# First inputs of the norm loaded a stage early, gates cast on ScalarE, rotary tables behind the first weights

## The chip, the core and the metric

The kernel runs on one core of a Trainium2 chip. The metric is device time in microseconds (us) of one launch, as the median of several runs. A profile shows one further execution. Engines are named as the profile names them: PE is TensorE (PEld its weight loads), DVE is VectorE, ACT is ScalarE, POOL is GpSimd, SP is SyncE, which only issues DMAs; SPq, ACTq and POOLq are DMA issues by these engines. L406 is line 406 of the kernel before.

## The reference, cut to what matters

Two transformer layers over 256 context rows and 1024 latent rows of width 1024, fp32 throughout. What the change touches is the modulation, the first norm, the projection, and the gates of the gated linear attention:

```python
for layer in range(DEPTH):
    m_lat = jnp.split((silu_c @ w_ada[layer] + b_ada[layer])[:, None, :], 6, axis=-1)
    m_ctx = jnp.split(silu_cc @ w_ada[layer] + b_ada[layer], 6, axis=-1)
    pl = project_heads(modulate(h_lat, m_lat[0], m_lat[1]) @ w_in[layer], ...)   # modulate: layer norm * (1 + scale) + shift
    pc = project_heads(modulate(h_ctx, m_ctx[0], m_ctx[1]) @ w_in[layer], ...)
    # in project_heads, per direction:
    gate = jax.nn.log_sigmoid((z @ w + b).astype(F32)) / GLA_GATE_NORM
    # rotary cos and sin are applied to the d_q, d_k, s_q, s_k columns only
    ...
    # three attentions (gla, diff, swa), out projection, post norm, swiglu
```

## The kernel before

The program is a row of stages with a barrier between each two: modulation; norm of the inputs; then per layer input projection (layer 1's follows layer 0's feed-forward), gated linear attention, differential attention, sliding-window attention, norm after attention, feed-forward. Within a stage each engine has its own instruction list, written by hand, and waits on semaphores. P is 128, D is 1024 and BANK is 512.

**Modulation** (`modulation`, L137). Six chunks of 512 columns of `w_ada` (2 MB each) go through a ring `W` of four buffers. SP issues a chunk (L160) and its four small bias pieces (L162); PE makes 32 small products of a chunk (L184); DVE adds the bias (L195); ACT sends the rows to the DRAM scratch `mod` (L171) and at the end waits for all of them.

**Norm of the inputs** (`norm_tiles` with kind "input"). Ten tiles of 128 rows. Step r of the software pipeline does on PE first the product of a `w_ada` chunk (L406, chunk r-1) and then the eight transposes of a tile (L414, tile r-1). SP loads chunk r (L350; from the third on after the product two earlier, since `aW` has two buffers), a bias row (L357) and tile r of the inputs into `hres` (L365, two buffers). DVE takes statistics (L432), ACT the deviation (L508), then normalizes (L514) for the transposes, then scales and shifts what PE turned (L528). The shift and scale columns come from `mod` by four POOL DMAs of single elements (L551); DVE waits for all four before anything else (L427), POOL too.

**Input projection** (`input_projection`). 21 weight tiles of 512 KB, two buffers: SP loads `raw` (L644), ACT casts it to the high part `whi` (L682), POOL subtracts for the low part `wlo` (L658), PE multiplies (L125 to L127 of the helper `product`). SP first issues the two rotary tables `cos` and `sin`, 1 MB each (L638, L639), and only then `raw`; POOL waits for both tables before its first subtraction. DVE uses them from tile 12 on.

**Gated linear attention** (`gated_linear_attention`). SP loads `zs` (six DMAs), then, once POOL has zeroed `wg`, its eight pieces (L925, L927), then `out` with the values (L928), the level tables into `X` (L929), keys and queries. PE makes five pairs of gate logits (L1016) in two PSUM buffers; ACT takes the absolute value (L1182) and DVE the minimum with 0 (L1296), which frees the buffer for the pair after next. DVE's list begins with the cast of the level tables (L1291). Then ACT does exp (L1185) and ln (L1188) of all five pairs; per pair j DVE subtracts (L1308, `g_done`) and casts the high part `ghi` (L1310), POOL makes the low part `glo` (L973). The distances (L1046, L1047) of piece k need `glo` of pair k, a free one of two `DP` buffers, and their exponentials (L1204) wait for all five `g_done`.

The few lines that set this order:

```python
# DVE, per pair j
dve.tensor_tensor(gate[:, j, :], gate[:, j, :], absx[:, j, :], ALU.subtract).then_inc(g_done, 1)
dve.wait_ge(g_done, j + 1)
dve.tensor_copy(ghi[:, 2 * j:2 * j + 2, :], gate[:, j, :]...).then_inc(ghi_done, 1)
# PE, distances: piece q waits for the exponential of piece q - 2
if q >= 2: pe.wait_ge(e_done, q - 1)
```

## Time and profile before

| | |
|---|---|
| three runs | 4027.97, 4030.92, 4032.74 us |
| median | 4030.92 us |
| the profiled execution | 4030.76 us; its span, first to last instruction, 4028.9 us |
| busy PE / POOL / DVE / ACT | 3537.6 / 1677.6 / 1615.7 / 1438.8 us (88 / 42 / 40 / 36%) |
| mean granted PE clock | 0.933 of full speed |
| modulation | 0 to 46.1 us, PE busy 18.3 |
| norm of the inputs | 46.1 to 148.4 us, PE busy 82.6 |
| input projection, layer 0 | 148.4 to 467.6 us, PE busy 292.4 |
| gated linear attention, layer 0 | from 467.6 us |
| input projection, layer 1 | 2268.5 to 2564.3 us |
| gated linear attention, layer 1 | from 2564.3 us |

The span is read stage by stage: between two barriers only the chain that ends last in a stage moves what follows. A timeline row gives the start of a piece of work, its length, and in brackets how long its engine sat idle before it and what released it.

### The profile page before, as it was taken

Reading aid. Unit: us, or ns where it says so; the run is one execution under the profiler, and the core shown is the slowest. Engines: PE = TensorE matmul, PEld = TensorE weight load, DVE = VectorE, ACT = ScalarE, POOL = GpSimd, SP = SyncE. Lnnn points to the kernel's source line nnn. Section 1 sums busy time; section 2 is a strip of 40 time slices with the busy share of each in tenths; the row PEclk is TensorE's granted clock in tenths of the full one; section 3 lists DMA queues with packets and bytes.
Section 4 is the critical chain, followed back from the end, with each engine's and each line's share of the span. In section 5 each row is a group of like instructions: output and inputs, shape, how many; then the busy total and the mean of one; then the engine's idle time right before and its main releaser. Section 6 shows DMA issues by size and latency. Waiting matters only on the chain. (4 is left out here: it accounts for less than half of the span.)

```text
span 4028.9 us, 54991 instructions
## 1 busy us (share of the span) xinstructions
PE 3537.6 (88%) x21518; PEld 2917.4 (72%) x21518; DVE 1615.7 (40%) x2566; ACT 1438.8 (36%) x2413; POOL 1677.6 (42%) x1108
## 2 busy tenths in 40 slices
PE   6799688698897999999999599597989879999997
PEld 2488578466576888888888488386665668888886
DVE  2103464585573222224433303564955722223324
ACT  2311265585543111113332211275854432222221
POOL 1211153493334444445555211243933345555553
PEclk8899789698998999999999799698999989999998
DMA  8422410231253222222333223312243533333332
GB/s 284 171 82 108 136 29 19 70 72 50 51 163 101 65 66 65 63 63 88 117 100 110 86 89 110 110 41 63 69 144 96 172 103 97 95 94 110 110 100 94
DMA packets 171083, 388.52 MB, mean 96 GB/s; under 512 B 14536, under 2 KB 75048, under 8 KB 170864
## 3 DMA queue, kind: packets, MB, share of 16 engines
q1 hardware_dynamic: 149184, 334.38, 27.2%
q10 hardware_dynamic: 19200, 44.63, 3.0%
q0 software_dynamic: 2480, 6.48, 0.6%
q8 instruction: 151, 2.47, 0.3%
q14 instruction: 68, 0.56, 0.0%
HBM read 319.41 MB, written 66.03 MB: 96 GB/s over the span
## 5 line engine op out<-in xcount | busy, mean ns | idle before, releaser
L2350 POOL TENSOR_TENSOR ffn_wlo<-ffn_raw,ffn_whi 128x1024 fp32r<-128x1024 f32 x264 | 644.5, 2448 | 680.8 <-ACT ffn_whi L2262 680.7
L2262 ACT CAST ffn_whi<-ffn_raw 128x1024 fp32r<-128x1024 f32 x264 | 272.6, 1049 | 879.0 <-PE ffn_acc L127 467.1
L2484 DVE TENSOR_TENSOR ffn_silu<-ffn_up,ffn_silu 128x256 f32<-128x256 f32 (+1 forms) x143 | 75.4, 528 | 946.3 <-PE ffn_up L127 937.0
L125 PE MATMUL ffn_gate<-second_uhi,ffn_whi 128*128 128x256 f32 (+1 forms) x1144 | 375.1, 328 | 42.9 <-POOL ffn_wlo L2350 34.3
L126 PE MATMUL ffn_gate<-second_ulo,ffn_whi 128*128 128x256 f32 (+1 forms) x1144 | 374.4, 327 | 0.0
L127 PE MATMUL ffn_gate<-second_uhi,ffn_wlo 128*128 128x256 f32 (+1 forms) x1144 | 374.1, 327 | 0.0
L125 PE MATMUL ffn_up<-second_uhi,ffn_whi 128*128 128x256 f32 (+1 forms) x1144 | 371.0, 324 | 0.9 <-POOL ffn_wlo L2350 0.9
L126 PE MATMUL ffn_up<-second_ulo,ffn_whi 128*128 128x256 f32 (+1 forms) x1144 | 370.8, 324 | 0.0
L127 PE MATMUL ffn_up<-second_uhi,ffn_wlo 128*128 128x256 f32 (+1 forms) x1144 | 370.4, 324 | 0.0
L2496 DVE TENSOR_TENSOR y<-ffn_acc,y 128x512 f32<-128x512 f32 x360 | 248.3, 691 | 260.3 <-PE ffn_acc L127 260.3
L125 PE MATMUL ffn_acc<-ffn_whi,ffn_hhi 128*128 128x512 f32 x792 | 315.0, 398 | 22.3 <-DVE y L2496 21.0
L126 PE MATMUL ffn_acc<-ffn_wlo,ffn_hhi 128*128 128x512 f32 x792 | 312.6, 395 | 0.0
L127 PE MATMUL ffn_acc<-ffn_whi,ffn_hlo 128*128 128x512 f32 x792 | 311.7, 394 | 0.0
L658 POOL TENSOR_TENSOR in_wlo<-in_raw,in_whi 128x1024 fp32r<-128x1024 f32 x42 | 100.2, 2389 | 454.1 <-ACT in_whi L682 454.1
L125 PEld LDWEIGHTS ffn_gate<-second_uhi,ffn_whi 128*128 128x128 f32 x1144 | 220.8, 193 | 64.4 <-POOL ffn_wlo L2350 35.1
L126 PEld LDWEIGHTS ffn_gate<-second_ulo,ffn_whi 128*128 128x128 f32 x1144 | 220.8, 193 | 19.1
L127 PEld LDWEIGHTS ffn_gate<-second_uhi,ffn_wlo 128*128 128x128 f32 x1144 | 220.7, 193 | 17.7
L125 PEld LDWEIGHTS ffn_up<-second_uhi,ffn_whi 128*128 128x128 f32 x1144 | 217.9, 190 | 18.9 <-POOL ffn_wlo L2350 1.5
L127 PEld LDWEIGHTS ffn_up<-second_uhi,ffn_wlo 128*128 128x128 f32 x1144 | 217.8, 190 | 17.3
L126 PEld LDWEIGHTS ffn_up<-second_ulo,ffn_whi 128*128 128x128 f32 x1144 | 217.9, 190 | 17.2
L2065 DVE TENSOR_SCALAR_CACHE_REDUCE diff_scores<-diff_scores 128x1280 f32<-128x1280 f32 (+1 forms) x144 | 196.8, 1384 | 34.9 <-PE diff_scores L1919 33.3
L125 PE MATMUL in_acc<-first_uhi,in_whi 128*128 128x512 f32 (+1 forms) x504 | 179.8, 357 | 20.7 <-POOL in_wlo L658 20.7
(285 smaller groups left out, 7980.1 us busy)
## 6 DMA issues: line engine op xcount, KB each, us to landing
ffn_raw<-w_ffn_dram SPq DMA_DIRECT2D x264, 512.0 KB, 3.6
in_raw<-w_in_dram SPq DMA_DIRECT2D x42, 512.0 KB, 3.6
norm_input_ada_w<-w_ada_dram SPq DMA_DIRECT2D x10, 2048.0 KB, 8.3
swa_ada_w<-w_ada_dram SPq DMA_DIRECT2D x8, 2048.0 KB
proj_scratch<-in_stage ACTq DMA_DIRECT2D x20, 640.0 KB, 2.9
ada_w<-w_ada_dram SPq DMA_DIRECT2D x6, 2048.0 KB
gla_kq<-proj_scratch SPq DMA_DIRECT2D x32, 320.0 KB
local_qhl<-heads_scratch SPq DMA_DIRECT2D x36, 256.0 KB
```

Of the source, the lines that this page charges most:

```text
L125: pe.matmul(out, st_hi, mv_hi, start=start, stop=False)
L126: pe.matmul(out, st_hi, mv_lo, start=False, stop=False)
L127: return pe.matmul(out, st_lo, mv_hi, start=False, stop=stop)
L658: pool.tensor_tensor(wlo[:, s, :, :], raw[:, s, :].rearrange("p (k n) -> p k n", k=KT), whi[:, s, :, :].bitcast(F32), ALU.subtract).then_i ...
L2065: dve.tensor_scalar(SC[:, c, 0:keys], SC[:, c, 0:keys], -scale, 3e38, ALU.mult, ALU.min, accum_out=ng[:, c:c + 1]).then_inc(neg_done, 1)
L2262: act.copy(whi[:, w % 3, :], raw[:, w % 2, :]).then_inc(w_hi, 1)
L2350: pool.tensor_tensor(wlo[:, w % 3, :], raw[:, w % 2, :], whi[:, w % 3, :].bitcast(F32), ALU.subtract).then_inc(w_ready, 1)
L2484: dve.tensor_tensor(sg[:, n % 2, 0:tn], UP[:, n % 2, 0:tn], sg[:, n % 2, 0:tn], ALU.mult).then_inc(mul_done, 1)
L2496: dve.tensor_tensor(Y[:, tt, cols], ACC[:, half, :], Y[:, tt, cols], ALU.add).then_inc(y_added, 1)
```

## The change

The kernel before is called before, the changed one after. The change has four parts.

First, new buffers `inputs_hres` and `inputs_ada_w` are allocated around modulation and norm. At the end of SP's list in modulation come the two context tiles (512 KB each) and the first two `w_ada` chunks of the norm (2 MB each). The norm no longer issues these four.

Second, in the input projection of both layers SP issues the first two weight tiles, then the two rotary tables, then the remaining weight tiles; from the second pair on in a loop, in layer 1 too, where they were unrolled. POOL's wait for the tables is gone.

Third, in the gated linear attention the eight pieces of `wg` are issued by ACT instead of SP.

Fourth, the cast `ghi` moves from DVE to ACT, one pair behind ln; the subtractions `glo` of pairs 1 and 3 move from POOL to DVE, and PE waits for `glo_pool` or `glo_dve`.

```diff
@@ -126,6 +126,16 @@
+
+
+def input_buffers(nc, ctx):
+    sb, _, sem = allocators(nc, ctx, "inputs_")
+    return {
+        "hres": sb("inputs_hres", [P, 2, D]),
+        "ada_w": sb("inputs_ada_w", [P, 2, KT, BANK]),
+        "h_in": [sem(f"h_in{s}") for s in range(2)],
+        "ada_in": [sem(f"ada_in{s}") for s in range(2)],
+    }
@@ -160,6 +170,11 @@
                     sp.dma_start(B[32 * j:32 * j + 2, n % 4, :], t["b_ada"][l:l + 1, part(c, j)].to_broadcast([2, P])).then_inc(w_in[n % 4], 16)
+            inputs = res["inputs"]
+            for s in range(2):
+                sp.dma_start(inputs["hres"][:, s, :], t["ctx"][s * P:(s + 1) * P, :]).then_inc(inputs["h_in"][s], 16)
+            for s in range(2):
+                sp.dma_start(inputs["ada_w"][:, s, :, :], t["w_ada"][1].rearrange("(k p) n -> p k n", p=P)[:, :, s * BANK:(s + 1) * BANK]).then_inc(inputs["ada_in"][s], 16)
@@ -228,7 +243,7 @@
         uhi, ulo, ident = res["uhi"], res["ulo"], res["ident"]
-        hres = sb(nm + "hres", [P, 2, D])
+        hres = sb(nm + "hres", [P, 2, D]) if post else res["inputs"]["hres"]
@@ -256,18 +271,18 @@
         if chunked:
-            aW = sb(nm + "ada_w", [P, 2, KT, BANK])
+            aW = res["inputs"]["ada_w"]
...
-        ada_in = [sem(f"ada_in{s}") for s in range(2)]
+        ada_in = [sem(f"ada_in{s}") for s in range(2)] if post else res["inputs"]["ada_in"]
...
         const_in, eps_set, one_plus = sem("const_in"), sem("eps_set"), sem("one_plus")
-        h_in = [sem(f"h_in{s}") for s in range(2)]
+        h_in = [sem(f"h_in{s}") for s in range(2)] if post else res["inputs"]["h_in"]
@@ -347,7 +362,7 @@
                         wait_apart(sp, product_done, chunk_count(i, r) - 2, sp_passed)
-                    sp.dma_start(aW[:, r % 2, :, :], columns).then_inc(ada_in[r % 2], 16)
+                        sp.dma_start(aW[:, r % 2, :, :], columns).then_inc(ada_in[r % 2], 16)
@@ -361,8 +376,9 @@
-                    wait_count(sp, summed if post else normed[1], count(i, r) - 2)
-                    sp.dma_start(hres[:, s, :], src_rows(i, s)).then_inc(h_in[s], 16)
+                    if post or not isinstance(i, int) or count(i, r) > 2:
+                        wait_count(sp, summed if post else normed[1], count(i, r) - 2)
+                        sp.dma_start(hres[:, s, :], src_rows(i, s)).then_inc(h_in[s], 16)
@@ -635,14 +651,14 @@
         def _(sp):
-            sp.dma_start(cos[:, :, :], t["rope_cos"].rearrange("a p n -> p a n")).then_inc(rope_in, 16)
-            sp.dma_start(sin[:, :, :], t["rope_sin"].rearrange("a p n -> p a n")).then_inc(rope_in, 16)
-
...
                 sp.dma_start(raw[:, s, :], t["w_in"][layer][bass.ds(n * P, P), :]).then_inc(raw_in[s], 16)
-            each_tile(sp, body)
+            each_tile(sp, body, 0, 1, False)
+            sp.dma_start(cos[:, :, :], t["rope_cos"].rearrange("a p n -> p a n")).then_inc(rope_in, 16)
+            sp.dma_start(sin[:, :, :], t["rope_sin"].rearrange("a p n -> p a n")).then_inc(rope_in, 16)
+            each_tile(sp, body, 1)
@@ -651,7 +667,6 @@
                 pool.dma_start(t["heads"][part, HEAD_SK:HEAD_SK + P, T:PAD_T], zero[:, :]).then_inc(pad_out, 16)
-            pool.wait_ge(rope_in, 32)
@@ -825,7 +840,7 @@
         logits, abs_done, exp_of_abs, log_done = sem("logits"), sem("abs_done"), sem("exp_of_abs"), sem("log_done")
-        g_done, ghi_done, glo_done = sem("g_done"), sem("ghi_done"), sem("glo_done")
+        g_done, ghi_done, glo_pool, glo_dve = sem("g_done"), sem("ghi_done"), sem("glo_pool"), sem("glo_dve")
@@ -919,12 +934,6 @@
                 sp.dma_start(zs[base + GATE_RANK:base + 2 * GATE_RANK, 0:1], proj[rows, T - 1:T]).then_inc(load["z"], 16)
-            sp.wait_ge(wg_zero, 1)
-            for base in (0, 64):
-                for d in range(2):
-                    sp.dma_start(wg[base + d * GATE_RANK:base + (d + 1) * GATE_RANK, :, d, :],
-                                 t["w_gate"][layer, d].rearrange("r (h k) -> r h k", h=H)).then_inc(load["w"], 16)
-                    sp.dma_start(wg[base + 32:base + 33, :, d, :], t["b_gate"][layer, d:d + 1, :].rearrange("a (h k) -> a h k", h=H)).then_inc(load["w"], 16)
@@ -968,10 +977,10 @@
             pool.wait_ge(zeroed, 2)
-            for j in range(PAIRS):
+            for j in range(0, PAIRS, 2):
...
                 pool.tensor_tensor(glo[:, 2 * j:2 * j + 2, :], gate[:, j, :].rearrange("p (c n) -> p c n", c=2),
-                                   ghi[:, 2 * j:2 * j + 2, :].bitcast(F32), ALU.subtract).then_inc(glo_done, 1)
+                                   ghi[:, 2 * j:2 * j + 2, :].bitcast(F32), ALU.subtract).then_inc(glo_pool, 1)
@@ -1040,7 +1049,7 @@
                     if g == 0:
-                        pe.wait_ge(glo_done, c // 2 + 1)
+                        pe.wait_ge(glo_dve if c // 2 % 2 else glo_pool, c // 4 + 1)
@@ -1177,15 +1186,29 @@
         def _(act):
+            act.wait_ge(wg_zero, 1)
+            for base in (0, 64):
+                for d in range(2):
+                    act.dma_start(wg[base + d * GATE_RANK:base + (d + 1) * GATE_RANK, :, d, :],
+                                 t["w_gate"][layer, d].rearrange("r (h k) -> r h k", h=H)).then_inc(load["w"], 16)
+                    act.dma_start(wg[base + 32:base + 33, :, d, :], t["b_gate"][layer, d:d + 1, :].rearrange("a (h k) -> a h k", h=H)).then_inc(load["w"], 16)
...
                 act.activation(absx[:, j, :], absx[:, j, :], ACT.Exp, scale=-1.0).then_inc(exp_of_abs, 1)
+
+            def high_part(j):
+                act.wait_ge(g_done, j + 1)
+                act.copy(ghi[:, 2 * j:2 * j + 2, :], gate[:, j, :].rearrange("p (c n) -> p c n", c=2)).then_inc(ghi_done, 1)
+
...
                 act.activation(absx[:, j, :], absx[:, j, :], ACT.Ln, bias=1.0).then_inc(log_done, 1)
+                if j:
+                    high_part(j - 1)
+            high_part(PAIRS - 1)
@@ -1306,8 +1329,10 @@
                 dve.tensor_tensor(gate[:, j, :], gate[:, j, :], absx[:, j, :], ALU.subtract).then_inc(g_done, 1)
-                dve.wait_ge(g_done, j + 1)
-                dve.tensor_copy(ghi[:, 2 * j:2 * j + 2, :], gate[:, j, :].rearrange("p (c n) -> p c n", c=2)).then_inc(ghi_done, 1)
+                if j >= 2 and j % 2 == 0:
+                    dve.wait_ge(ghi_done, j)
+                    dve.tensor_tensor(glo[:, 2 * j - 2:2 * j, :], gate[:, j - 1, :].rearrange("p (c n) -> p c n", c=2),
+                                      ghi[:, 2 * j - 2:2 * j, :].bitcast(F32), ALU.subtract).then_inc(glo_dve, 1)
@@ -2545,14 +2570,16 @@
         everything = list(range(TILES))
-        modulation(nc, t, res)
...
                     operand(ctx, "first")
-                    norm_tiles(nc, t, res, "input", layer, everything, False)
+                    with nc.cleanup_on_exit(), ExitStack() as inputs:
+                        res["inputs"] = input_buffers(nc, inputs)
+                        modulation(nc, t, res)
+                        norm_tiles(nc, t, res, "input", layer, everything, False)```

SP, from the last chunk of modulation into the norm, before:

```order
L160 DMA ada_w<-w_ada_dram 128x8x512
L162 DMA ada_b<-b_ada_dram 2x128 x4
L134 UNCONDITIONAL_BRANCH
L332 UNCONDITIONAL_BRANCH
L350 DMA norm_input_ada_w<-w_ada_dram 128x8x512
L365 DMA norm_input_hres<-ctx_dram 128x1024
L350 DMA norm_input_ada_w<-w_ada_dram 128x8x512
L357 DMA norm_input_ada_b<-b_ada_dram 2x512
L365 DMA norm_input_hres<-ctx_dram 128x1024
```

and after:

```order
L170 DMA ada_w<-w_ada_dram 128x8x512
L172 DMA ada_b<-b_ada_dram 2x128 x4
L175 DMA inputs_hres<-ctx_dram 128x1024 x2
L177 DMA inputs_ada_w<-w_ada_dram 128x8x512 x2
L144 UNCONDITIONAL_BRANCH
L347 UNCONDITIONAL_BRANCH
L372 DMA norm_input_ada_b<-b_ada_dram 2x512
L365 DMA inputs_ada_w<-w_ada_dram 128x8x512
```

The branches are the stage's end and the next one's start: four large loads have moved ahead of them, and the first large load of the norm is now its third chunk.

ACT, from the start of the gated linear attention of layer 0 to its first exponentials, before:

```order
L1178 UNCONDITIONAL_BRANCH
L1182 ACTIVATE gla0_E<-gla0_unit 128x1024 x5
L1185 ACT_TABLE_LOAD
L1185 ACTIVATE gla0_E<-gla0_E 128x1024 x5
L1188 ACT_TABLE_LOAD
L1188 ACTIVATE gla0_E<-gla0_E 128x1024 x5
L1204 ACT_TABLE_LOAD
L1204 ACTIVATE gla0_E<-gla0_dist 128x2x2x128 x13
```

and after, from the load of the table for ln on:

```order
L1208 ACT_TABLE_LOAD
L1208 ACTIVATE gla0_E<-gla0_E 128x1024 x2
L1204 CAST gla0_ghi<-gla0_XAB 128x1024
L1208 ACTIVATE gla0_E<-gla0_E 128x1024
L1204 CAST gla0_ghi<-gla0_XAB 128x1024
L1208 ACTIVATE gla0_E<-gla0_E 128x1024
L1204 CAST gla0_ghi<-gla0_XAB 128x1024
L1208 ACTIVATE gla0_E<-gla0_E 128x1024
L1204 CAST gla0_ghi<-gla0_XAB 128x1024 x2
L1227 ACT_TABLE_LOAD
L1227 ACTIVATE gla0_E<-gla0_dist 128x2x2x128 x13
```

`gla0_XAB` holds the gates and `gla0_E` the logarithms. The five casts now stand between the logarithms and ahead of the table for the exponentials; no further table load has come in.

## Rows read from the trace of the kernel before

**Rows 1.** Timeline, modulation to norm: start, length (us), work [idle before <-releaser].

```profile
25.63 4.59 SPq L162 DMA_DIRECT2D ada_b<-b_ada_dram  x4
...
43.18 1.16 ACTq L171 DMA_DIRECT2D mod_scratch<-ada_rows  x4
...
46.12 0.39 SPq L350 DMA_DIRECT2D norm_input_ada_w<-w_ada_dram  x1
...
49.51 0.88 POOL L551 DMA_DIRECT2D norm_input_scale<-mod_scratch  x1
...
56.65 9.50 PE L406 MATMUL norm_input_ada_acc<-norm_input_ada_w,silu_c 128*2 128x512 f32 x16 [14.82 <-DMA norm_input_ada_w<-w_ada_dram]
56.67 0.17 DVE L427 TENSOR_SCALAR norm_input_scale<-norm_input_scale 128x16 f32<-128x16 f32 x1 [13.53 <-DMA norm_input_scale<-mod_scratch]
...
57.92 1.29 DVE L432 BATCH_NORM_STATS2 norm_input_stats<-norm_input_hres 128x6 f32<-128x512 f32 x2 [1.08 <-DMA norm_input_hres<-ctx_dram]
...
61.68 1.24 ACT L514 ACTIVATE norm_input_x<-norm_input_hres,norm_input_nmu,norm_input_rstd 128x1024 f32<-128x1024 f32 x1 [0.42 <-DVE norm_input_nmu L445]
...
66.08 1.09 PE L414 MATMUL norm_input_tr<-ident,norm_input_x 128*128 128x128 f32 x8
...
67.10 7.03 PE L406 MATMUL norm_input_ada_acc<-norm_input_ada_w,silu_c 128*2 128x512 f32 x16
```

**Rows 2.** Table of stretches, DMA alone busy: stretch, then busy times, PEclk, DMA share, GB/s.

```profile
30.00:35.00 5.00, 2.83 (x76) 2.07 (x72) 1.15 (x4) 0.00 (x0) 0.00 (x0) 0.84 1.05 405
```

**Rows 3.** Timeline, TensorE after a pause in the norm after attention.

```profile
1129.96 0.76 PE L125 MATMUL norm_attention_y<-norm_attention_wohi,norm_attention_mhi 128*128 128x512 f32 x1 [2.44 <-POOL norm_attention_mlo L564]
```

**Rows 4.** Timeline, start of both input projections; last, landing of their weights.

```profile
148.42 0.41 SPq L638 DMA_DIRECT2D in_cos<-rope_cos_dram  x1
...
158.02 1.04 ACT L682 CAST in_whi<-in_raw 128x1024 fp32r<-128x1024 f32 x1 [14.13 <-DMA in_raw<-w_in_dram]
...
161.62 0.79 PE L125 MATMUL in_acc<-first_uhi,in_whi 128*128 128x512 f32 x1 [20.67 <-POOL in_wlo L658]
...
2278.24 1.04 ACT L682 CAST in_whi<-in_raw 128x1024 fp32r<-128x1024 f32 x1 [13.59 <-DMA in_raw<-w_in_dram]
...
DMA to landing us min/median/max: 3.4/3.6/9.5
```

**Rows 5.** Timeline, start of the gated linear attention, layer 0.

```profile
470.29 0.74 SPq L925 DMA_DIRECT2D gla_wg<-w_gate_dram  x1
...
475.75 0.44 SPq L928 DMA_DIRECT2D gla_out<-proj_scratch  x1
...
476.94 3.79 PE L1016 MATMUL gla_unit<-gla_wg,gla_z 33*128 33x512 f32 x8 [22.93 <-DMA gla_wg<-b_gate_dram]
...
483.41 0.76 DVE L1291 CAST gla_levels<-gla_X 128x1152 fp32r<-128x1152 f32 x1 [21.41 <-DMA gla_X<-gla_levels_dram]
...
484.42 2.35 DVE L1296 TENSOR_SCALAR gla_XAB<-gla_unit 128x1024 f32<-128x1024 f32 x2
```

**Rows 6.** Timeline, its gates; last row, the same place in layer 1.

```profile
499.48 1.28 ACT L1188 ACT_TABLE_LOAD   x1
500.77 4.84 ACT L1188 ACTIVATE gla_E<-gla_E 128x1024 f32<-128x1024 f32 x5
501.94 1.22 DVE L1308 TENSOR_TENSOR gla_XAB<-gla_XAB,gla_E 128x1024 f32<-128x1024 f32 x1 [3.07 <-ACT gla_E L1188]
...
508.94 2.71 DVE L1310 CAST gla_ghi<-gla_XAB 128x1024 fp32r<-128x1024 f32 x1
...
516.70 1.08 ACT L1204 ACTIVATE gla_E<-gla_dist 128x512 f32<-128x512 f32 x2 [6.77 <-DVE gla_XAB L1308]
...
519.51 2.34 POOL L973 TENSOR_TENSOR gla_glo<-gla_XAB,gla_ghi 128x1024 fp32r<-128x1024 f32 x1 [0.63 <-DVE gla_ghi L1310]
...
522.00 0.55 PE L1046 MATMUL gla_dist<-gla_levels,gla_ghi 128*128 128x256 f32 x1 [1.78 <-POOL gla_glo L973]
...
2618.70 0.55 PE L1046 MATMUL gla_dist<-gla_levels,gla_ghi 128*128 128x256 f32 x1 [1.78 <-POOL gla_glo L973]
```

1 line of the change is left out of this document (added).

## The prediction, made before the changed kernel was run

> **What bounds the kernel now.** I read the table of stages first: nearly everything is a stage in which PE is busy nine tenths of the time, and the change touches none of that work. It touches three kinds of stage starts, where PE idles, so I read the timeline there. At the start of the norm of the inputs PE waits 14.82 us for its first chunk of weights and starts at 56.65, with the stage open since 46.12; DVE waits until 56.67 for the shift and scale columns [rows 1]. At the start of a projection ACT casts the first weights at 158.02, 9.6 us after SP's first issue at 148.42, because 2 MB of tables went ahead, and PE starts at 161.62 [rows 4]. At the start of the linear attention DVE waits until 483.41 for the level tables and PE until 476.94 for the gate weights [rows 5]; then a pair of gates costs DVE a subtraction of 1.22 and a cast of 2.71 while POOL works beside it, and the last low part starts only at 519.51 [rows 6]. The reader is to see that each wait ends a chain that the whole stage hangs on.
>
> **Norm of the inputs.** Removed: four loads of 5 MB from the stage's start. They now follow the sixth chunk on SP's queue. The DMA engines move 405 GB/s there [rows 2]. The first six chunks hold 12.6 MB and, at that rate from about 6 us on, are through by 37 (an estimate from that rate); 5.2 MB more take 12.9 us, so the queue drains at about 49.8, and the first chunk of the norm, 1 MB of tiles ahead of it, is there at about 45. SP finished its issues at 30.22 and the stage ended after 43 [rows 1], so SP has 12 us for four more. The six chunks stand ahead in the queue and are not delayed.
>
> What is delayed are the last rows that ACT sends at 43.18 to 44.34; the next stage opened 1.8 us after that [rows 1]. They now land beside a running 2 MB load. Bounds: 0, and about 5 us, from the columns that POOL issued until 50.39 and that came at 56.67 beside a load, 6.28 us, against the 1.8 or less that the rows take now [rows 1]. I take 1.2, near the short end, since the rows are eight descriptors and the columns thousands.
>
> In the norm PE can take its first chunk at once: 46.3 + 9.50 = 55.8. The first transposes need the columns too. POOL still issues them until 50.39. Lower bound for their landing is some 1.8 us more, as for the rows; upper bound is 56.67 as now. I take 53.0: the load beside them is gone by 49.8. From there the chain measured from the statistics at 57.92 to the end of the normalization at 61.68 + 1.24 is 5.0, and the addition ahead of it 0.2: 58.2. With the 1.2 us of the rows that is 59.4 where the row of the first transposes has 66.08: a gain of 6.7. Everything later in the stage follows at PE's pace: chunk of 7.03 and transposes of 1.09, and the third chunk is issued when the first product ends, 9 us before PE wants it, as now.
>
> PE then pauses 2.4 us between its first chunk and the transposes, where before it went straight on. The chunk in the granted clock's lower level (1.2 GHz of 2.4) took 9.50 against 7.03, so one more fall costs up to 2.5 [rows 1]. After a pause of 2.44 us elsewhere PE came back with a first product of 0.76 us, slow [rows 3]. I charge 1.2, between 0 and 2.5. **Term: 6.7 - 1.2 = 5.5, between 0 and 9.**
>
> **Input projection, both layers.** The first weight tile takes the place of the tables at 148.42. Landing takes 3.4 to 3.6 us where nothing is ahead [rows 4]: 152.0 instead of 158.02. The second follows 1.3 later, as now. The tables then land at about 158.5; POOL no longer waits for them, DVE first uses them twelve tiles later, and the third weight tile, issued when POOL has finished its first at about 155.6, lands behind them at 160, while PE has two tiles of some 14 us each to do (292.4 us for 21). The loop that replaces unrolled issues costs SP nothing that is seen: SP waits for POOL there. **Term: 6.0 in each layer, 12.0; between 5 and 6.5 each.** The rows of layer 1 are the same, 9.7 after the issue.
>
> **Linear attention, first half, both layers.** Eight issues leave SP's list: 475.75 - 470.29 = 5.46 us [rows 5]. `out` and the level tables are issued and land that much earlier, 483.41 becomes 478.0, and DVE's first minimum 484.42 becomes 479.0. For that the absolute value of pair 0 must be there, 3.1 us after PE's start (half of PE's 3.79 for two pairs and about 1 each for ACT and the hand-overs [rows 5]). ACT issues the eight pieces at the same 0.68 each from about 468.2 to 473.6, and PE starts 1.2 after the last one now: 474.9, or 475.5 with a little contention. The gain is whole as long as PE starts by 475.9. Here the row shows eight issues that hold up all behind them for 5.4 us. The Trainium skill says in "DMA: Bandwidth & Descriptors", "Issuing engines are not separate DMA queues", that issuing on several engines "will only save the time on the sequencer it takes to initiate the DMA, which is usually small relative to the DMA itself". By that sentence this half would bring next to nothing; the row speaks against it, as these pieces hold only a few KB. **Term: 5.4 in each layer, 10.8.**
>
> **Second half, both layers.** Counted from the first ln at 500.77 [rows 6]. Now the pairs follow at DVE's 1.2 + 2.7 = 3.9 each and the last low part ends at 519.51 + 2.34 = 21.1. After: an ln is 0.97 and a cast on ACT 1.04, as for the weights [rows 4]. ACT does ln 0, ln 1, then cast 0 when the first subtraction is there at 2.4; so cast 0 ends at 3.5, cast 1 at 5.5, cast 2 at 7.55, cast 3 at 9.6, cast 4 at 10.95 (its subtraction ends at 9.85). DVE has two low parts of 1.22, ending at 7.05 and 11.1; POOL three of 2.34, the last from 11.0 to 13.4. Then the load of the table for exp, which lay in a pause, stands behind cast 4: 1.28, so the first exponential starts at 12.25 against 516.70, that is 15.9. Three more pieces follow in PE's steps of 1.2: the last piece of the first step starts at 15.25, where the row has 522.00, that is 21.2. What is late next is PE itself, as pieces wait for a `DP` buffer, not the low part (13.4). Gain 5.95, and layer 1 has the same row, 2618.70. Bounds: 1, if ACT's casts take the 2.71 that DVE's took (rival b), and 6.5. **Term: 5.9 in each layer, 11.8.**
>
> Whether ACT's cast stays at 1.04 beside DVE and POOL has no row here; the cast of the weights, taken while no other engine worked, is the nearest in kind.
>
> **Sum.** 5.5 + 12.0 + 10.8 + 11.8 = 40.1. Against the profiled execution, 4030.76 us: 3990.7. The median of the runs is 4030.92, the same; I say 3990.7.
>
> **Rivals.** (a) Small transfers suffer beside the large ones. For it: the columns' 6.28 us [rows 1]. If the gate weights take that after 473.6, PE starts at 479.9 and the first half brings 1.4 instead of 5.4 in each layer: 8 us less. If the last rows of modulation take 5, 3.8 less. Both: 4002.5; one: 3995 to 3999. Against it: the pieces of `wg` have few descriptors, and now land 1.2 after their last issue though `out` is issued right behind them [rows 5]. The Trainium skill, in "DMA: Bandwidth & Descriptors", "Queues, rings and completion order", says that an engine drains a whole packet of one queue before it turns to the next; that would be such a delay, and no row here shows its size.
>
> (b) ACT is the new bound in the gates. If its casts took 2.71 as DVE's did, a pair would cost 0.97 + 2.71 = 3.7 against 3.9 and the second half would bring about 1 in each layer: 4000.5. A smaller form: the table load has to wait for the cast to drain. The rows show none: the load at 499.48 has no idle time of ACT ahead of it, right behind the five exponentials, and ln starts as its 1.28 are over [rows 6]. If a drain as long as the load came behind the cast, 1.28 in each layer, the time would be 3993.3. The Trainium skill, "ScalarE: Activation LUTs", "What ACT_TABLE_LOAD costs", counts about 1.38 us of drain with every switch; by that 3993.5.
>
> (c) The early loads buy nothing, because the columns bound the norm's start as they do now (56.67 against 56.65): the chain then gives 56.67 + 5.2 + 1.2 = 63.1, the first term is about 2, and the time 3994.
>
> (d) Slower. The granted clock moves against the change: PE's busy stretches of the feed-forward, 2000 us long, start in another phase. One fall costs 2.5 us at most [rows 1]. To lose the 40 us and 8 more it takes 20 more falls than now; with 24 the time is 4050.7. Nothing in the profile ties such falls to a shift of a whole stage.
>
> **How the numbers follow.** A difference of 0.2%, 8 us, is about what a measurement of this kernel tells from none. Forecast, 3985 to 3995: 0.70. (a) 0.09, (b) 0.08 (of it 0.03 for the small form), (c) 0.08, (d) 0.02, and 0.03 for a loss that has no place here. The forecast, (c), the small form of (b) and part of (a) lie within 3983 to 4001, which I take as the range. All but (d) and the unplaced loss are faster: 0.95 faster, 0.03 the same, 0.02 slower.
>
> **What would show it.** In the profile after: first product of the norm within 0.5 us of the stage's opening, first transposes 7 us earlier; modulation ending by about 47; first cast of weights 3.6 us after SP's first issue in both projections; first minimum of the gates 5.4 earlier after the stage's opening; five casts on ACT of about 1.04; first exponential some 11.5 us after the first ln. I am wrong if the next stage after modulation opens beyond 49, if the gate logits start later than 8.5 us after the stage opens, or if DVE and ACT wait for each other in the gates so that the first exponential comes later than 14 us after the first ln.

## The result and the profile after

The changed kernel takes 4001.62 us (median of four runs, 3997.66 to 4006.36) where the kernel before takes 4030.45 (four runs): 28.8 us less, ratio 0.9929 with a 95% interval of 0.9912 to 0.9946. The profiled execution of after took 4000.35 us with a span of 3998.6. The forecast was 3990.7, a gain of 40.1. The direction is right; more than a quarter of the gain is missing, and the time lies just beyond the upper end of the range, 4001. In all runs compared here the mean granted clock of TensorE was 0.93 to 0.94 of full speed; the one run far below that, at 0.725 and 4630.99 us, belongs to the last kernel of the experiments and is left out of its median.

Two lists find the missing part. The first is the length of each stage, from barrier to barrier, in the profiled executions:

| us | modulation | norm | projection 0 | linear attention 0 | projection 1 | linear attention 1 | all other stages | span |
|---|---|---|---|---|---|---|---|---|
| before | 46.1 | 102.3 | 319.2 | 251.2 | 295.8 | 212.7 | 2801.6 | 4028.9 |
| after | 49.8 | 93.4 | 312.6 | 244.2 | 289.7 | 208.7 | 2800.2 | 3998.6 |

The stage of the linear attention is over 200 us long and its later part moves by some us from run to run with the granted clock: the unaltered after kernel, profiled once more, had 249.5 where this table has 244.2, with the same gates. From DVE's first weighing to the stage's end it took 199.1 us at a mean granted clock of 0.90 there, and 193.0 us at 0.94 here. So the second list reads fixed places in it, in us after the stage opened (POOL's first row):

| us after opening, layer 0 / layer 1 | before | after |
|---|---|---|
| PE's first gate product | 9.3 / 9.8 | 12.2 / 11.6 |
| DVE's first minimum | 16.8 / 16.8 | 15.3 / 14.8 |
| ACT's first ln | 33.2 / 33.2 | 31.7 / 31.1 |
| ACT's first exponential of the distances | 49.1 / 49.1 | 46.7 / 46.1 |
| DVE's first weighing of keys and queries | 56.3 / 56.2 | 51.1 / 50.6 |

The gain, term by term: norm 5.2 (predicted 5.5), projections 6.6 + 6.1 (predicted 12.0), first half of the gates 1.5 + 2.0 (predicted 10.8; to the first minimum), second half 3.6 + 3.6 (predicted 11.8; from the first ln to the first weighing). The sum is 28.6, of the 30.3 by which the two profiled spans differ and beside 28.8 in the medians. That it comes so near is in part luck. In layer 0 the stage is 7.0 shorter, more than the 5.1 gained at the weighing, and in the second profile of after only 1.7; in layer 1, 4.0 of the 5.6 gained at the weighing are left at the stage's end. What is missing against the forecast stands in the two terms of the linear attention.

**Norm.** Timeline of after where [rows 1] are of before: start, length, work, and in brackets the idle time before it and its releaser.

```profile
26.48 18.43 ACTq L186 DMA_DIRECT2D mod_scratch<-ada_rows  x16
...
49.79 0.10 POOL L562 MEMSET norm_input_eps<- 128x1 f32 x1 [49.33 <-POOLq L144]
49.83 9.98 PE L422 MATMUL norm_input_ada_acc<-inputs_ada_w,silu_c 128*2 128x512 f32 x16 [7.43 <-PEq L144]
...
53.17 0.88 POOL L567 DMA_DIRECT2D norm_input_scale<-mod_scratch  x1
56.09 0.17 DVE L443 TENSOR_SCALAR norm_input_scale<-norm_input_scale 128x16 f32<-128x16 f32 x1 [12.37 <-DMA norm_input_scale<-mod_scratch]
...
61.22 1.09 PE L430 MATMUL norm_input_tr<-ident,norm_input_x 128*128 128x128 f32 x8 [1.41 <-ACT norm_input_x L530]
...
62.24 7.03 PE L422 MATMUL norm_input_ada_acc<-inputs_ada_w,silu_c 128*2 128x512 f32 x16
```

PE starts 0.04 us after the stage opens instead of 10.5. The columns land 2.04 after their last issue is over (53.17 + 0.88 to 56.09), against 6.28 before beside a load. The price is ahead of it: the last rows of modulation are issued until 44.91 and the stage ends 4.88 later; before, that was 1.78. The transposes are at 61.22, 4.9 earlier than in [rows 1].

**Projection.** The same view where [rows 4] are of before:

```profile
143.22 0.85 SPq L657 DMA_DIRECT2D in_raw<-w_in_dram  x2
...
147.16 1.04 ACT L697 CAST in_whi<-in_raw 128x1024 fp32r<-128x1024 f32 x1 [8.85 <-DMA in_raw<-w_in_dram]
```

The first cast comes 3.94 us after SP's first issue, where it came 9.60 after it; in layer 1 it is 4.36 (2245.82 to 2250.18), where it was 9.7. PE starts 5.7 and 5.4 earlier after the opening. The rest of the 6.6 and 6.1 lies in the products themselves, 291.54 us in all instead of 292.39 and 263.44 instead of 264.20; the granted clock in PE's first 20 us was 0.90 and 0.91 against 0.85 and 0.87 before.

**Start of the linear attention.** The same view where [rows 5] are of before, and then the table of stretches (busy time of PE, PEld, DVE, ACT and POOL, then clock, DMA share and GB/s) of the time in which PE waits:

```profile
458.86 0.49 SPq L937 DMA_DIRECT2D gla_out<-proj_scratch  x1
...
459.39 0.72 SPq L938 DMA_DIRECT2D gla_X<-gla_levels_dram  x1
...
460.16 5.34 SPq L943 DMA_DIRECT2D gla_kq<-proj_scratch  x8
...
461.25 0.64 ACTq L1194 DMA_DIRECT2D gla_wg<-b_gate_dram  x1
...
467.06 0.76 DVE L1314 CAST gla_levels<-gla_X 128x1152 fp32r<-128x1152 f32 x1 [16.84 <-DMA gla_X<-gla_levels_dram]
...
467.96 3.79 PE L1025 MATMUL gla_unit<-gla_wg,gla_z 33*128 33x512 f32 x8 [25.74 <-DMA gla_wg<-b_gate_dram]
...
471.13 1.22 DVE L1319 TENSOR_SCALAR gla_XAB<-gla_unit 128x1024 f32<-128x1024 f32 x1 [2.98 <-ACT gla_E L1197]
```

```profile
461.00:463.00 2.00, 0.00 (x0) 0.00 (x0) 0.00 (x0) 0.00 (x0) 0.00 (x0) 0.50 0.96 389
463.00:465.00 2.00, 0.00 (x0) 0.00 (x0) 0.00 (x0) 0.00 (x0) 0.00 (x0) 0.50 1.01 407
```

ACT has issued the last piece of `wg` at 461.89, but PE starts at 467.96, 6.07 later; in layer 1 5.7 later (2541.41 to 2547.12). In [rows 5] it was 1.2. In between the DMA engines are full, with values, levels, keys and queries at 389 to 407 GB/s; before, while the last pieces were issued (474 to 476), they were nearly idle at 13 GB/s. In the seven profiles whose linear attention starts with these lists the 6.07 is 5.6 to 6.3, and 4.6 to 5.8 in layer 1. What DVE waits for is no longer the level tables but ACT's absolute value, behind PE. The tables are cast 11.3 us after the opening, 4.6 earlier than before, where the prediction had 10.4.

**Gates.** Where [rows 6] are of before: after on DVE, then ACT, then POOL.

```profile
488.65 2.36 DVE L1331 TENSOR_TENSOR gla_XAB<-gla_XAB,gla_E 128x1024 f32<-128x1024 f32 x2 [3.08 <-ACT gla_E L1208]
492.01 2.54 DVE L1331 TENSOR_TENSOR gla_XAB<-gla_XAB,gla_E 128x1024 f32<-128x1024 f32 x1 [1.00 <-ACT gla_E L1208]
494.48 1.21 DVE L1334 TENSOR_TENSOR gla_glo<-gla_XAB,gla_ghi 128x1024 fp32r<-128x1024 f32 x1
495.61 4.50 DVE L1331 TENSOR_TENSOR gla_XAB<-gla_XAB,gla_E 128x1024 f32<-128x1024 f32 x2
```

```profile
487.49 2.00 ACT L1208 ACTIVATE gla_E<-gla_E 128x1024 f32<-128x1024 f32 x2
...
496.86 1.05 ACT L1204 CAST gla_ghi<-gla_XAB 128x1024 fp32r<-128x1024 f32 x1 [0.27 <-DVE gla_XAB L1331]
500.14 1.04 ACT L1204 CAST gla_ghi<-gla_XAB 128x1024 fp32r<-128x1024 f32 x1 [2.24 <-DVE gla_XAB L1331]
501.21 1.28 ACT L1227 ACT_TABLE_LOAD   x1
502.50 1.08 ACT L1227 ACTIVATE gla_E<-gla_dist 128x512 f32<-128x512 f32 x2
```

```profile
491.13 2.35 POOL L982 TENSOR_TENSOR gla_glo<-gla_XAB,gla_ghi 128x1024 fp32r<-128x1024 f32 x1 [30.72 <-ACT gla_ghi L1204]
495.71 3.32 POOL L982 TENSOR_TENSOR gla_glo<-gla_XAB,gla_ghi 128x1024 fp32r<-128x1024 f32 x1 [2.23 <-ACT gla_ghi L1204]
```

The casts on ACT take the predicted 1.04, and no idle time stands between the last one and the table load. But DVE's third subtraction takes 2.54 instead of 1.22, and the fourth and fifth together 4.50. Laid over POOL's rows, the lengths add up to taking turns: POOL works from 491.13 to 493.48, and DVE's subtraction that began at 492.01 ends at 494.55, about 1.1 after that. POOL's next, 3.32 long, begins 0.10 after a subtraction of DVE; 3.32 is about the rest of that subtraction (1.0) and 2.34. The last cast waits 2.24 for DVE, and the first exponential comes 15.0 us after the first ln, where 12.25 was predicted and 15.9 stood before.

A far smaller instruction, in the norm of the same trace, shows that this is waiting and not working at half speed:

```profile
74.07 2.33 DVE L461 SCALAR_TENSOR_TENSOR norm_input_nmu<-norm_input_mv,norm_input_rstd 128x1 f32<-128x1 f32 x1
74.04 2.34 POOL L585 TENSOR_TENSOR first_ulo<-norm_input_x,first_uhi 128x1024 fp32r<-128x1024 f32 x1 [5.56 <-DVE first_uhi L496]
```

It has one element per partition and takes 0.16 in the median of its ten; here it ends within 0.02 us of POOL's subtraction. Not every DVE instruction waits: the addition at 66.28, with one operand in PSUM, takes 0.68 while POOL subtracts from 66.14 to 68.48, and 0.67 at 76.32, where POOL is done.

### The profile page after: what moved, and what is told of

Read it like the earlier page. It is cut to its first block and busy times, and to the rows that moved or that the text cites. A ratio compares the mean times of both kernels' runs of the same rounds, so it can differ in the third digit from the quotient of the medians.

```text
span 3998.6 us, 55066 instructions
## 1 busy us (share of the span) xinstructions
PE 3531.9 (88%) x21518; PEld 2912.4 (73%) x21518; DVE 1602.3 (40%) x2560; ACT 1449.1 (36%) x2423; POOL 1662.3 (42%) x1104
## 5 line engine op out<-in xcount | busy, mean ns | idle before, releaser
L125 PE MATMUL ffn_gate<-second_uhi,ffn_whi 128*128 128x256 f32 (+1 forms) x1144 | 375.4, 328 | 42.8 <-POOL ffn_wlo L2375 34.1
L125 PE MATMUL ffn_up<-second_uhi,ffn_whi 128*128 128x256 f32 (+1 forms) x1144 | 370.9, 324 | 0.8 <-POOL ffn_wlo L2375 0.8
L125 PE MATMUL ffn_acc<-ffn_whi,ffn_hhi 128*128 128x512 f32 x792 | 314.1, 397 | 22.4 <-DVE y L2521 21.2
L125 PEld LDWEIGHTS ffn_gate<-second_uhi,ffn_whi 128*128 128x128 f32 x1144 | 221.0, 193 | 64.3 <-POOL ffn_wlo L2375 34.9
L125 PEld LDWEIGHTS ffn_up<-second_uhi,ffn_whi 128*128 128x128 f32 x1144 | 217.8, 190 | 18.9 <-POOL ffn_wlo L2375 1.5
L2068 POOL TENSOR_TENSOR diff_w<-diff_w,diff_e 128x1280 f32<-128x1280 f32 (+1 forms) x72 | 192.0, 2666 | 6.0
```

The costliest lines, as they stand in the source:

```text
L125: pe.matmul(out, st_hi, mv_hi, start=start, stop=False)
L2068: pool.tensor_tensor(w, w, E[:, u % 4, 0, 0:keys], ALU.add).then_inc(w_done, 1)
```

## Experiments

Each is an edit of the changed kernel. Times of a single run are given beside the run of before on the same chip; since runs of one and the same kernel lie up to 13 us apart (3996.44 to 4009.6 below), the places in the stages decide, and the time only supports them.

Two theories stand behind the first five; a third, of the same kind as T for the last rows of modulation, is called M in the expectations. **T**: the pieces of `wg` and other small transfers land late because large loads run beside them, not because of their engine or their count. **P**: a DVE instruction of two SBUF operands (or DVE's cast) and a POOL subtraction exclude each other; ACT's casts have no part in it. The rivals are in the expectations.

### Gate weights issued by SP again

```diff
 # SP, ahead of the load of the values; removed from ACT's list
+            sp.wait_ge(wg_zero, 1)
+            for base in (0, 64):
+                for d in range(2):
+                    sp.dma_start(wg[...], t["w_gate"][...]).then_inc(load["w"], 16)
+                    sp.dma_start(wg[...], t["b_gate"][...]).then_inc(load["w"], 16)
```

> The changed kernel with one part undone: SP issues the eight pieces of wg again, ahead of out and the level tables. Both theories expect the two linear-attention stages to open as they did before up to the first gates: PE's first logits 9.3 us and DVE's first minimum 16.8 us after the stage opens (after: 12.2 and 15.3; layer 1: 11.6 and 14.8). Theory T (the pieces on ACT land late because they run beside the loads that now start 5.4 us earlier): the move is worth 1.5 to 2 us in each layer, time 3 to 4 us above the changed kernel. Rival (the move is worth what the prediction gave it and something else in the stage ate it): 5.4 in each layer, 11 us above.

Measured: 4002.9 us (before 4029.84). PE's first gate product comes 9.5 and 9.4 after opening, the first minimum 17.1 and 17.2, against 15.3 and 14.8 in after. The third part of the change is worth 1.7 and 2.4 us, not 5.4. Over the seven profiles that have its lists, the minimum comes 14.7 to 15.7 and 13.7 to 15.2 after opening, so it is worth 1.4 to 2.4 and 2.0 to 3.5.

### Gate weights landed before the large loads start

```diff
+            sp.dma_start(X[:, 2, 0:tables * P].rearrange("p (l n) -> p l n", n=P), t["gla_levels"]).then_inc(load["lv"], 16)
+            sp.wait_ge(load["w"], 128)
             sp.dma_start(out[:, :, :], proj[T_GV * P:(T_GV + 2) * P, 0:T].rearrange("(i p) n -> p i n", p=P)).then_inc(load["v"], 16)
-            sp.dma_start(X[:, 2, 0:tables * P].rearrange("p (l n) -> p l n", n=P), t["gla_levels"]).then_inc(load["lv"], 16)
```

> The changed kernel, but SP issues the level tables before out and then waits until the eight pieces of wg have landed before it issues out, keys and queries; nothing large runs beside the pieces but the 0.6 MB of tables. Theory T (contention of the pieces with out and keys on the DMA engines): PE's first logits 7.4 to 8.4 us after the stage opens instead of 12.2, first minimum at about 10.5 to 11.5 instead of 15.3, some 4 us less in each layer, 8 in all. Rival (ACT's queue lands its pieces 6 us late whatever runs beside them): first logits stay at about 12, first minimum at 15, and out and keys come later, so the time rises by 0 to 4 us.

Measured: 3992.38 us (before 4029.84). Its timeline:

```profile
459.74 0.64 ACTq L1195 DMA_DIRECT2D gla_wg<-b_gate_dram  x1
461.54 0.76 DVE L1315 CAST gla_levels<-gla_X 128x1152 fp32r<-128x1152 f32 x1 [12.69 <-DMA gla_X<-gla_levels_dram]
462.15 0.39 SPq L939 DMA_DIRECT2D gla_out<-proj_scratch  x1
...
462.22 3.78 PE L1026 MATMUL gla_unit<-gla_wg,gla_z 33*128 33x512 f32 x8 [21.37 <-DMA gla_wg<-b_gate_dram]
```

The same eight pieces, from the same engine, land 1.84 us after the last issue (460.38 to 462.22) instead of 6.07, with only the 0.6 MB of level tables beside them; in layer 1 it is 2.4. The first minimum is at 11.0 and 11.4 after opening. That is T, and 5.9 and 5.4 earlier than in before: the size that was predicted for this half, by another order. The weighing is at 46.8 and 47.2 (51.1 and 50.6 in after), so the later keys and queries cost nothing.

### Casts on DVE and low parts on POOL again

```diff
-                if j >= 2 and j % 2 == 0:
-                    dve.wait_ge(ghi_done, j)
-                    dve.tensor_tensor(glo[pair j - 1], ...).then_inc(glo_dve, 1)
+                dve.wait_ge(g_done, j + 1)
+                dve.tensor_copy(ghi[:, 2 * j:2 * j + 2, :], gate[:, j, :].rearrange("p (c n) -> p c n", c=2)).then_inc(ghi_done, 1)
```

ACT's `high_part` is gone, and POOL makes all five low parts.

> The changed kernel with the fourth part undone: casts on DVE, all five low parts on POOL. From the first ln: first exponential at 15.9 us and DVE's first weighing at 23.1 as before (after: 15.0 and 19.45). Theory P (DVE's subtractions and POOL's low parts take turns, so the gates' chain is the sum of both engines' work; the cast alone left it): the part is worth 3.6 us at the first weighing and 3 to 4.5 at each stage's end, time 6 to 9 us above the changed kernel. Rival (it is worth the 5.9 of the prediction, hidden by noise of the clock): 12 us above.

Measured: 4014.78 us (before 4029.84), that is 14.4 above the profiled run of after, where 6 to 9 were expected: the stages of the linear attention are 5.7 and 4.3 longer, the others, which the edit doesn't touch, 4.4. The 5.7 shows nothing of the edit, as the second profile of after has the same length, 249.5 against 249.8 here. From the first ln to the first exponential it is 15.9 again and to the weighing 23.1, against 15.0 and 19.5 in after; the fourth part is worth 3.6 in each layer. DVE's and POOL's rows of this kernel:

```profile
489.71 0.69 DVE L1326 CAST gla_ghi<-gla_XAB 128x1024 fp32r<-128x1024 f32 x1
490.32 1.22 DVE L1324 TENSOR_TENSOR gla_XAB<-gla_XAB,gla_E 128x1024 f32<-128x1024 f32 x1
491.58 2.72 DVE L1326 CAST gla_ghi<-gla_XAB 128x1024 fp32r<-128x1024 f32 x1
```

```profile
490.58 3.16 POOL L982 TENSOR_TENSOR gla_glo<-gla_XAB,gla_ghi 128x1024 fp32r<-128x1024 f32 x1 [30.15 <-DVE gla_ghi L1326]
...
506.03 2.34 POOL L982 TENSOR_TENSOR gla_glo<-gla_XAB,gla_ghi 128x1024 fp32r<-128x1024 f32 x1 [0.63 <-DVE gla_ghi L1326]
```

Here the cast that [rows 6] show with 2.71 is seen without POOL beside it: 0.69. The 2.72 of the next one is the wait until POOL ends at 493.74 and then 0.56. POOL's 3.16 is about the rest of DVE's subtraction (0.9) and 2.34.

### All low parts on DVE

```diff
 # DVE, behind the subtraction of pair j; POOL makes none
+                for k in [[], [0], [1], [2], [3, 4]][j]:
+                    low_part(k)
```

> The changed kernel with all five low parts on DVE, the low part of pair j-1 behind the subtraction of pair j, none on POOL. Theory P (a DVE subtraction of two SBUF operands and a POOL subtraction take turns): every DVE subtraction and low part takes 1.22 us, none 2.5 to 4.5; the casts on ACT stay 1.04. By the lists then the first exponential comes 13.35 us after the first ln (15.0 in the changed kernel) and DVE's first weighing about 17.8 after it (19.45). Rival A (what stretches DVE's subtractions is ACT's cast or ln beside them, reading the same tiles): subtractions of 2.5 us and more remain, the first exponential 15 or later. Whole time 3997 to 3999 by P, 4002 or more by A, beside what the clock adds.

Measured: 3995.3 us (before 4030.67). DVE's rows:

```profile
487.61 2.36 DVE L1332 TENSOR_TENSOR gla_XAB<-gla_XAB,gla_E 128x1024 f32<-128x1024 f32 x2 [3.07 <-ACT gla_E L1204]
489.95 1.23 DVE L1326 TENSOR_TENSOR gla_glo<-gla_XAB,gla_ghi 128x1024 fp32r<-128x1024 f32 x1
491.09 1.22 DVE L1332 TENSOR_TENSOR gla_XAB<-gla_XAB,gla_E 128x1024 f32<-128x1024 f32 x1
492.23 1.22 DVE L1326 TENSOR_TENSOR gla_glo<-gla_XAB,gla_ghi 128x1024 fp32r<-128x1024 f32 x1
```

With POOL silent all twenty DVE instructions of the two layers take 1.22 to 1.23, with ACT's casts among them. The first exponential is 12.8 after the first ln, the weighing 17.25, each half a us sooner than expected. P holds and A falls. DVE does three instructions more than in after and is done sooner.

### Low parts on DVE, out of the way of the subtractions

```diff
+                for k in [[], [], [0], [], [1, 2, 3, 4]][j]:
+                    low_part(k)
```

> The changed kernel with all five low parts on DVE, but only that of pair 0 among the subtractions (behind subtraction 2), the other four behind subtraction 4, so that no low part stands ahead of a subtraction that ACT waits for. Theory P: first exponential 12.25 us after the first ln, the number that was predicted for the changed kernel (15.0 in it); DVE's first weighing 16.8 to 17.0 after it (19.45); PE's last piece of the first step at about 15.3. Rival A (ACT's casts stretch DVE's subtractions): as the changed kernel, 15.0 and 19.4. Whole time by P about 5 less than the changed kernel, 3996, beside what the clock adds; by A 4001.

Measured: 3994.79 us (before 4030.67). First exponential 11.95 after the first ln, the weighing 16.4 after it, in both layers. The prediction's schedule for ACT (12.25) is right once nothing excludes DVE.

### One weight chunk of the norm loaded in modulation

```diff
-            for s in range(2):
+            for s in range(1):
                 sp.dma_start(inputs["ada_w"][:, s, :, :], ...).then_inc(inputs["ada_in"][s], 16)
 # norm, SP: chunk 1 is issued at the stage's start again
```

> The changed kernel, but only the two context tiles and the first chunk are loaded in modulation; the second chunk (2 MB) is issued at the start of the norm. After: modulation ends at 49.8, first transposes at 61.2, norm ends at 143.2. Theory M (the last rows of modulation land late because 2 MB more are still in the queues): the queue drains at about 45, modulation ends at 46.5 to 47.3; the columns are slowed beside the second chunk and land at 53 to 55; first transposes at 58.5 to 60.5, norm ends 1 to 2.7 us earlier than 143.2. Rival (the end of modulation moved for another reason, such as the added instructions or the new buffers): modulation still ends at about 49.8 and the norm ends later than 143.2.

Measured: 4002.97 us (before 4029.84). Modulation ends at 47.64, 2.1 earlier than in after; but its last row was issued until 43.14, 1.8 earlier, and still lands 4.5 after that. The expected end of 46.5 to 47.3 was missed. In the norm:

```profile
47.64 0.38 SPq L367 DMA_DIRECT2D inputs_ada_w<-w_ada_dram  x1
...
51.03 0.88 POOL L569 DMA_DIRECT2D norm_input_scale<-mod_scratch  x1
...
57.78 0.17 DVE L445 TENSOR_SCALAR norm_input_scale<-norm_input_scale 128x16 f32<-128x16 f32 x1 [15.83 <-DMA norm_input_scale<-mod_scratch]
...
62.91 1.97 PE L432 MATMUL norm_input_tr<-ident,norm_input_x 128*128 128x128 f32 x8 [6.54 <-ACT norm_input_x L532]
64.81 8.65 PE L424 MATMUL norm_input_ada_acc<-inputs_ada_w,silu_c 128*2 128x512 f32 x16
```

Beside this one load the columns land 5.87 after their last issue instead of 2.04. PE then stood idle 6.54 us (1.41 in after), and its transposes and second chunk are slow, 1.97 and 8.65 against 1.09 and 7.03. The norm takes 100.5 and ends at 148.1 instead of 143.2; 1 to 2.7 us earlier than 143.2 was expected. Both chunks ahead of the norm are the better choice in spite of the rows.

### Only the tiles loaded in modulation

```diff
-            for s in range(2):
-                sp.dma_start(inputs["ada_w"][:, s, :, :], ...).then_inc(inputs["ada_in"][s], 16)
 # norm, SP: both chunks are issued at the stage's start again
```

> The changed kernel with only the two context tiles (1 MB) loaded in modulation; both weight chunks of the norm are issued in the norm again. Theory M (the last rows of modulation land late because large loads still run beside them): the queue drains by about 40, the last rows are issued by 44.3 as before, modulation ends at 46.1 (46.12 before, 49.79 in the changed kernel). Rival N (the lag is that of the end of the stage with two more buffers or semaphores, not of a load): 49 or more. The norm's start then is as before: first product 10 us after opening, columns beside a load 10.5 after opening, norm about 102 long, so the sum of modulation and norm about 148.2 against 143.2 in the changed kernel; whole time about 4006.

Measured: 4008.41 us (before 4030.67). The last row is issued until 43.31 and modulation ends at 45.1, 1.8 later, as in before, with the two new buffers in place: so it is the weight loads that hold the rows up, and N falls. PE starts at 55.69, 10.6 after opening; the transposes come at 64.99, and the norm takes 102.8. Modulation and norm sum to 147.9 (143.2 in after, 148.4 before).

### Both repairs together, beside the changed kernel

The edits of the second and the fifth experiment in one kernel; the changed kernel once more; and the former with the second weight chunk issued by SP in the norm once the columns have landed (`sp.wait_ge(const_in, const_loads)` ahead of it).

> The changed kernel unaltered, timed beside the two that follow, on the same chip. Every theory expects 4001 to 4002.

> The changed kernel with both repairs: SP issues the level tables first and waits for the gate weights before it issues the values, keys and queries; and all low parts on DVE, that of pair 0 behind subtraction 2 and the rest behind subtraction 4. If the two losses are separate and add, DVE's first weighing comes 4.0 earlier by the first (51.1 to 46.8 and 50.6 to 47.2 after the stage's opening) and 3.0 earlier by the second (19.45 to 16.4 after the first ln): 43.8 and 44.2 after the opening, and the whole time is 2 times 7 under the changed kernel: 3987 to 3989. Rival: the second gain is eaten by keys and queries that now land too late for the weighing; then weighing stays at 46 or later and the time at 3991 to 3994.

> As combined, and only the first weight chunk of the norm is loaded in modulation; SP issues the second in the norm once the four column loads have landed. Theory M (rows of modulation and columns of the norm each suffer from the large load beside them): modulation ends at 47.6 as with one chunk, the columns land 2.0 after the last issue as in the changed kernel, the second chunk is there before PE has turned the first tile, so the sum of modulation and norm is 141.2 against 143.2 in the changed kernel and 148.1 with one chunk issued at once. Rival: the second chunk comes too late, PE waits for it, and the sum is 143 or more. Whole time 2 under combined, or the same.

| | median us | runs | ratio to before on the same chip, 95% interval |
|---|---|---|---|
| before | 4027.24 | 9, 4025.59 to 4034.77 | |
| the changed kernel again | 4001.95 | 5, 3996.44 to 4009.6 | 0.9929, 0.9915 to 0.9942 |
| both repairs | 3989.03 | 4, 3986.89 to 3989.9 | 0.9898, 0.9883 to 0.9913 |
| and one chunk late | 3995.86 | 4, 3988.21 to 3998.11 | 0.9914, 0.9898 to 0.9929 |

With both repairs every run is faster than the fastest of the changed kernel (3989.9 against 3996.44); the medians are 12.9 us apart and the weighing is at 43.7 and 44.0 after opening, where 43.8 and 44.2 were expected. The losses were separate and add; this version beats both kernels.

The last variant missed. Modulation ends at 47.5 and the columns land 2.2 after their last issue, as expected, but:

```profile
53.89 0.38 SPq L368 DMA_DIRECT2D inputs_ada_w<-w_ada_dram  x1
...
56.65 0.37 SPq L365 DMA_DIRECT2D inputs_ada_w<-w_ada_dram  x1
...
59.00 0.35 SPq L384 DMA_DIRECT2D inputs_hres<-x_dram  x1
...
62.07 8.59 PE L425 MATMUL norm_input_ada_acc<-inputs_ada_w,silu_c 128*2 128x512 f32 x16 [1.95 <-DMA inputs_ada_w<-w_ada_dram]
...
68.83 1.29 DVE L451 BATCH_NORM_STATS2 norm_input_stats<-inputs_hres 128x6 f32<-128x512 f32 x2 [4.07 <-DMA inputs_hres<-x_dram]
```

The chunk lands 8.2 after its issue, with the third chunk sent after it at 56.65, and the third tile waits behind both and is 9.8 under way. The norm takes 97.8, 3.6 more than with both repairs alone (94.2), while modulation gained 2.1: the rival of that expectation, 145.2 for the sum against 143.8.

## Why the prediction came out as it did

**Norm: the sum right, two sizes in it off.** The step "I take 1.2, near the short end, since the rows are eight descriptors" failed: modulation ends 3.67 later, of which 0.57 is later issuing and 3.10 the landing. The reason given, few descriptors, decided nothing. Against it the clock's fall, charged at 1.2, did not come: PE paused 1.41 where 2.4 was predicted, and the second chunk took 7.03 at a granted clock of 1.00. Other profiles of the same lists had the predicted pause and more, 2.88 and 2.91, and the chunk took 7.03 all the same. The slow product after 2.44 us, [rows 3], did not carry over to this place. The columns landed 6.30 after opening (6.7 predicted), and from there to the transposes it was 5.1 (5.2). Net 5.2 for 5.5: that it is so near is luck, as the two errors, 2.5 too little for the rows and 1.2 too much for the clock, stand against each other and against a few tenths elsewhere. Rival (c), columns as late as 56.67, did not happen in its sense: they gate the start, but come 2.04 after the issue.

**Projection: right.** 6.6 and 6.1 for 6.0 each, with the 6.6 a little beyond the term's 6.5. The first cast alone moved by 5.7 and 5.3, and PE's start by 5.7 and 5.4; the 0.85 and 0.76 by which the products were shorter, beside a higher granted clock, were no part of the sum. That POOL, SP's loop and the later tables would cost nothing was right too. The clue was that both chains, [rows 4], had only one thing in front.

**Linear attention, first half: the mechanism right, the landing mis-sized.** SP issues `out` 5.1 us earlier after the opening, and the levels are cast 4.6 and 4.3 earlier, 5.4 by the prediction. The failed step is "PE starts 1.2 after the last one now: 474.9, or 475.5 with a little contention". The 1.2 was measured at a time when nothing large was under way (13 GB/s): on one queue, `wg` stood ahead of `out`. The change put `out`, levels, keys and queries in flight before the last `wg` piece. With 6.07 and 5.7 in the place of 1.2, this half is worth 1.5 and 2.0 instead of 5.4. It is rival (a), which had the size of layer 0 almost exactly: 1.4. It was given 0.09, against its own evidence of 6.28 in [rows 1]. The Trainium skill's sentence in "DMA: Bandwidth & Descriptors", "Issuing engines are not separate DMA queues", that a second issuing engine saves usually little beside the DMA itself, came nearer to this outcome (1.7 and 2.4 us by the first experiment) than the prediction's row did; yet the issue time was not small, 5.4, and the second experiment got all of it. What cost it was the order of arrival. The Trainium skill, in the same page's section "Queues, rings and completion order", has packets of one queue drained before the next is served; the 6.07 and the 1.84 are in line with that, but no run here shows single packets.

**Second half: the failed step is side by side.** "DVE has two low parts of 1.22 ... POOL three of 2.34" placed them beside each other and beside DVE's subtractions. They take turns. The cast on ACT, its 1.04, the table load without a drain and the pace of PE behind it were all right, and rival (b) was wrong in both forms. The evidence stood in [rows 6]: a cast of 2.71 for 1024 elements beside a subtraction of 1.22 for the same number was read as a price of the cast. It is 0.69 and a wait of about 2 for POOL. The trace of before shows both, a few rows ahead of those in [rows 6], first DVE and then POOL:

```profile
503.19 0.69 DVE L1310 CAST gla_ghi<-gla_XAB 128x1024 fp32r<-128x1024 f32 x1
...
505.06 2.71 DVE L1310 CAST gla_ghi<-gla_XAB 128x1024 fp32r<-128x1024 f32 x1
```

```profile
504.07 3.16 POOL L973 TENSOR_TENSOR gla_glo<-gla_XAB,gla_ghi 128x1024 fp32r<-128x1024 f32 x1 [31.86 <-DVE gla_ghi L1310]
```

Read so, the rows say that moving the cast away leaves DVE's subtractions as the next to wait. The term was 3.6 per layer instead of 5.9: the last piece of the first step starts 17.6 us after the first ln, where 15.25 was predicted and 21.2 stood before. The Trainium skill says it in "SBUF — State Buffer", in the section "SBUF: two separate sides": GpSimd and a DVE instruction with two SBUF inputs, or one in a 2-port perf mode, share a port pair under an exclusive lock, held for the whole instruction by the one that starts first. The trace agrees for the subtractions: 2.54 beside POOL and 1.22 without it. The cast has one input and waits too; that it runs in such a mode no run here shows. The prediction did not weigh that page.

**The signs.** All three signs of being wrong that the prediction named came: the norm opened at 49.8 (beyond 49), the gate logits started 12.2 and 11.6 after the opening (beyond 8.5), and the first exponential came 15.0 after the first ln (beyond 14).

**Range.** The losses of both halves came together, 7.3 and 4.6 us, while the range reached to one rival at a time. By the bounds of the terms the gain could be 5.7 larger (3.5 + 1.0 + 1.2), so that nothing led below 3985, but 25 smaller (5.5 + 2.0 + 8.0 + 9.8), and 3983 to 4001 hid that.

**Open.** The size of modulation's lag. In the eight profiles of kernels with the same code there, modulation ended between 48.0 and 49.8, but always 4.8 to 5.0 us after its last row was issued; what moved was the issue, which was over between 43.2 and 44.9. With one chunk queued the lag was 4.5 in one kernel and 3.1 in the other, and both ended at about the same time, 47.6 and 47.5, after the DMA engines had fallen from 380 GB/s to under 185 between 44 and 45. That weight loads cause the lag is shown; what sets 4.9 while they run is not.

## What to carry to other kernels

A landing time read from a trace belongs to what else was in flight: before a small, urgent transfer is moved to another engine's queue, list what will now be issued ahead of it, and hold the large loads back by a wait on it if they are not needed first. An instruction that is twice as long as its like elsewhere in the trace may hold a wait inside it: look which engine ends just before it does, before pricing its removal by its length. And when POOL subtracts in SBUF while DVE has instructions with two SBUF operands, or such casts, add their times; giving all of it to the faster one (1.22 against 2.34 here) can be quicker than sharing.

## What the runs showed that was not expected

- Three extra instructions on DVE made DVE's part shorter: the weighing came 17.25 us after the first ln with all low parts on DVE and 19.45 with POOL making three of five.
- Eight small pieces took 1.84 us to land with little beside them and 6.07 beside loads at about 400 GB/s; the columns 2.04 and 5.87; the last rows of modulation 1.8 and 4.9. Three kinds of small transfer, 3 to 4 us each.
- After TensorE's pause before the transposes, 1.41 to 2.91 us long in the eight profiles with both chunks loaded early, the second chunk took 7.03 in each; after one of 6.54 it took 8.65. Two pauses of 2.47 and 1.95 with only the transposes between them, in the last kernel, gave 8.59. Tables of stretches, PEclk third from the end, of the second chunk: after, and then the kernel with one chunk.

```profile
62.30:69.00 6.70, 6.70 (x17) 1.21 (x16) 1.60 (x4) 4.33 (x10) 2.34 (x1) 1.00 0.92 353
```

```profile
65.00:73.00 8.00, 8.00 (x16) 1.32 (x14) 3.00 (x7) 4.24 (x10) 2.35 (x1) 0.81 0.10 40
```

The mean is 1.00 (2.4 GHz throughout) against 0.81, part of the stretch at 1.2 GHz.
